# Seven depthwise jobs as seven block products each, and the block sums of h made in the value stage

## The chip, the cores and the metric

The kernel runs on one core of a Trainium2 chip. Time is the device's, in microseconds (us), from the first to the last instruction of one execution; several executions give a median. PE is TensorE, DVE is VectorE, ACT is ScalarE, POOL is GpSimd, and SP is the queue of SyncE, which here only issues transfers.

## The reference

Two transformer blocks on one sequence of 512 rows of width 1024. What the change touches is in the first block, here cut to it:

```
h = rmsnorm(x, pre_g) * (1 + sc) + sh                  # 512 x 1024
parts = split(h @ w_in)                                # b_gate, c_gate, x_in, z_a, q, k, v, z_b, g_a, g_b
q, k = rope(q), rope(k)
attn = neighbourhood_attention(q, k, v, k_ctx, v_ctx, rpb)
y_a = (silu(z_a) * b_gate * dwconv3(c_gate * x_in, conv_w, conv_b)) @ w_out_conv
y_b = (silu(z_b) * attn) @ w_out_attn
y = (sigmoid(g_a) * y_a + sigmoid(g_b) * y_b) @ w_o
x = x + gt * rmsnorm(y, post_g)
```

`dwconv3` is a depthwise convolution over three neighbouring rows. The second block (differential and forget-gate attention, memory attention, an MLP) follows and is not changed.

## The kernel before

All weights come as jobs of 1 MB: 1024 rows by 256 columns, as a tile `raw` of 128 partitions x 8 x 256. Each matmul operand is held as a high part (rounded to fp32r) and a low part (the rest), and a product is three matmuls: high by high, high by low, low by high (`mm3`). So a job is split before use: ACT makes the high part `wh` (`split_hi`, L314) and DVE or POOL the low part `wl` (`split_job`, L320). `raw`, `wh` and `wl` have two buffers each, so the split of a job runs while PE works on the job before it. SP loads `raw` in the order of the jobs, each load behind the split of the job two before (L418, L419).

An ordinary job (`tiles_job`) makes two output tiles of 128 x 512, each from 8 x 3 matmuls of 512 columns, into the two PSUM banks `acc`. A job as seven block products (`seven`) cuts weights and data into 2 x 2 blocks and makes seven products of 4 x 3 matmuls of 256 columns where eight would be needed. For that DVE makes four sums of weight blocks (`weight_sums`), ACT their high parts (`sums_hi`) and DVE their low parts (`sums_lo`), POOL makes the low parts of three plain weight blocks (`quads_lo`), and DVE puts the products together (L2053 to L2080). It also needs four sums of blocks of the data, split once for all its jobs.

The stages of the first block run in this order. **Value stage**: four jobs of six groups each (`token_group`, 24 matmuls of 256 columns into one bank); ACT evacuates each group (L1173), and stands between group 1 and group 2 to make the high part of the next job. **QK and attention**, with POOL making the rope sums and biases. **Depthwise stage**: sixteen jobs in turns of four (c_gate, x_in, b_gate, z_a), all ordinary, in loops of the hardware; job 0 is spread over the last attention steps. POOL meanwhile scales four gate weight tiles and sums them (L2542, L2549); nothing needs these sums before the next stage. **z_b stage**, four ordinary jobs. **Gate stage**: eight ordinary output jobs and then eight jobs g_a and g_b as seven products; POOL makes the sums of h (`gate_combos`, L2569 to L2578) while the output jobs run, from the high and the low part of h added again.

In SP's queue stand, after the first loads: a wait for h (`h_ready`) and for a small memset by POOL (`relb_ready`), seven small loads of tables, and then the loop of weight loads from value job 2 on. The tables go to `farena`, where x0 (from which h is made) lay; the tables are used after the value stage.

Of the kernel before, what the change touches and what calls it, by code (L numbers as in the profile page):

```python
# [8 lines left out]
SEQ = 512  # L9
KT = D // 128  # L10
GW, GR = 64, 8
CTX = 256
# [58 lines left out]
def build(nc, A, out):  # L71
# [3 lines left out]
    with ctx:  # L75
# [13 lines left out]
        small = sb("small", [128, 176])  # L89
# [14 lines left out]
        rarena = sb("rarena", [128, R_KB * 256], f32r)  # L104

# [26 lines left out]
        kx = [R(104, SEQ + 128 + CTX), R(111, SEQ + 128 + CTX)]  # L132
        cin = R(32, KT, SEQ)
        og = R(64, KT, SEQ)
        merged = R(96, KT, SEQ)
        wmod_a = view(early, 0, (8, KT, 256))
# [25 lines left out]
        hquads, hcombos = view(early, 32, (2, 2, 4, 256)), view(early, 48, (4, 4, 256))  # L162
        ht = view(rarena, 32, (4, 4, 256)), view(rarena, 48, (4, 4, 256))
# [33 lines left out]
        p1_t, u_q, w_q, v_q = F(16, 256), F(17, 256), F(18, 256), F(19, 256)  # L197
# [85 lines left out]

        def gate_home(c):
            kb = 112 if c == 0 else (76, 64)[c % 2]
            return tuple(view(rarena, kb + 6 * x, (3, 4, 128)) for x in range(2))
# [4 lines left out]

        def s_job(it, q0, c):
            return it * 4 + (14 + 4 * q0 + c)

        def acts(sj):
            return sj * 2 - 20
# [89 lines left out]
        def _(sp):  # L386
# [18 lines left out]
            sp.wait_ge(s_("h_ready"), KT)  # L405
            sp.wait_ge(s_("relb_ready"), 1)
# [26 lines left out]
        def _(pe):  # L433
# [420 lines left out]
            hold(pe, "xc_lo", 4)  # L854
            for c in range(8):
                seven(0, base + 8 + c, g + 16 + 2 * c, c, gate_home(c), gate_x)
# [6 lines left out]
            late_rows(0, JB["WO"], GB["WO"], merged, "merged_ready", 0)  # L863
            for c in range(1, 4):
                tiles_job(0, 2, JB["WO"] + c, 2, GB["WO"] + 2 * c, merged, between=memory_sum if c == 2 else None)
# [129 lines left out]
            for i in range(6):  # L995
                seven(0, JB["GO2"] + 6 + i, GB["GO2"] + 20 + 2 * i, 8 + i, gate2_home(i), gate2_x)
# [93 lines left out]
        def _(act):  # L1090
# [176 lines left out]
            def conv_turn(it, turn):  # L1267
                jb, gb, m0 = JB["CONV"] + 4 * turn, GB["CONV"] + 8 * turn, 2 * turn
                for c in range(4):
                    if c == turn == 0:  # L1270
                        split_hi(act, it, 4, jb + 2)
                        continue
                    if c == 1 - turn:
                        act.wait_ge(s_("gate_free"), it + turn + 1)
                        act.dma_start(gate_w, A["gate"][bass.ds(it + turn, 1)].rearrange("a p k n -> (a p) k n")
                                      if turn else A["gate"][0]).then_inc(s_("gate_in"), 16)
                    for t in range(2):
                        g = gb + 2 * c + t
                        if c == 0:
                            conv_first(it, turn, t)  # L1280
                        if c == 1:
                            wait_evacuated(act, it, 8, g)
                            f(y_t[:, t], u_t[:, t], ACT.Identity, bias=par[:, bass.ds(it * 2 + (P_CB + m0 + t), 1)],
                              scale=par[:, bass.ds(it * 2 + (P_CW + 8 + m0 + t), 1)]).then_inc(s_("tap_ready"), 1)
                        if c == 3:
                            acc_wait_ready(act, it, 8, g)
                            f(sg_t[:, t], acc[g % 2][:], ACT.Sigmoid).then_inc(s_("zsig_ready"), 1)
                    if c == 2:
                        acc_wait_ready(act, it, 8, gb + 5)
                    if c < 3:  # L1290
                        split_hi(act, it, 4, jb + c + 2)
                for t in range(2):
                    act.wait_ge(s_("cinf_ready"), it * 2 + (m0 + t + 1))
                    f(cin[0][:, bass.ds(it * 2 + (m0 + t), 1)].rearrange("p a n -> p (a n)"), y_t[:, t], ACT.Copy)\
                        .then_inc(s_("cin_hi"), 1)
                split_hi(act, it, 4, jb + 5)

            conv_turn(0, 0)
            with act.Fori(0, 3) as it:
                conv_turn(it, 1)  # L1300
# [25 lines left out]
            def prepare_first(it, base):  # L1326
                s = base % 2
                act.wait_ge(s_(f"raw_loaded{s}"), loads(it, base))
                f(wh[:, s, :, 0:128], raw[:, s, :, 0:128], ACT.Copy)
                f(quadrant(wh[:, s], 1, 1), quadrant(raw[:, s], 1, 1), ACT.Copy).then_inc(s_("hi_done"), 1)  # L1330

            def sums_hi(base, sj, home):
                for n in range(4):
                    hold(act, "sums_ready", sj * 4 + (2, 3, 3, 4)[n])
                    f(sum_home(0, base, n, home), bank(SUMS[n]), ACT.Copy).then_inc(c_("wsum_hi"), 1)

            def copy_p1(g, sj):
                hold(act, "prod_done", sj * 5 + 1)
                f(p1_t, acc[g % 2][:, 0:256], ACT.Copy).then_inc(c_("p1_copied"), 1)

# [14 lines left out]
            def merged_hi(c):  # L1355
                for t in (1, 0):
                    act.wait_ge(s_("mf_ready"), 2 * c + 2 - t)
                    f(merged[0][:, 2 * c + t], ya[:, 2 * c + t], ACT.Copy).then_inc(s_("merged_hi"), 1)
# [3 lines left out]
            for c in range(8):  # L1362
                if c < 7:
                    split_hi(act, 0, 2, jb + c + 1)
                else:
                    prepare_first(0, jb + 8)
                    sums_hi(jb + 8, 0, gate_home(0))
# [4 lines left out]
                if c == 5:  # L1372
                    hold(act, "combo_ready", 8)
                    for n in (0, 2, 1, 3):
                        f(ht[0][:, n], hcombos[:, n], ACT.Copy).then_inc(c_("xc_hi"), 1)
            for c in range(8):
# [3 lines left out]
                copy_p1(g, c)  # L1380
                if c < 7:
                    sums_hi(base, c + 1, gate_home(c + 1))
                else:
                    split_hi(act, 0, 2, base)
                quads_through(0, g, c, ACT.Sigmoid, lambda t: None)
# [211 lines left out]
            for n in range(4):  # L1597
# [5 lines left out]
                else:  # L1603
                    prepare_first(0, base + 1)
                    sums_hi(base + 1, 8, gate2_home(0))
# [4 lines left out]
                for u in range(4):  # L1610
# [5 lines left out]
                    for x in {(1, 3): (0, 2), (2, 0): (1,), (2, 1): (3,)}.get((n, u), ()):  # L1616
                        hold(act, "combo_ready", 16)
                        f(ht2[0][:, x], hcombos2[:, x], ACT.Copy).then_inc(c_("xc_hi"), 1)
            for i in range(6):
                base, g, sj = JB["GO2"] + 7 + i, GB["GO2"] + 20 + 2 * i, 8 + i  # L1620
                if i < 5:
                    prepare_first(0, base)
                copy_p1(g, sj)
# [100 lines left out]
            def finish(t, c, it, q0, sj):  # L1724
                hold(act, "relu_done", sj * 2 + 2 - t)
# [4 lines left out]
            def seven(it, c, q0, jb, gb):  # L1730
# [3 lines left out]
                copy_p1(g, sj)  # L1734
# [13 lines left out]
            def combos_hi(*which):  # L1748
                for x, made in which:
                    if made:  # L1750
                        hold(act, "combo_ready", 16 + made)
# [33 lines left out]
        def _(v):  # L1785
# [182 lines left out]

            v.wait_ge(s_("lo_done"), JB["CONV"] + 2)
            with v.Fori(0, 4) as it:  # L1970
                own.loop(it, 4)
                for c in range(4):
                    g = GB["CONV"] + 2 * c
                    if c == 0:
                        acc_wait_ready(v, it, 8, g + 1)
                    for t in range(2):
                        if c == 1:
                            wait_evacuated(v, it, 8, g - 2 + t)
                            acc_wait_ready(v, it, 8, g + t)
                            free_acc(tt(u_t[:, t], acc[(g + t) % 2][:], c_t[:, t], MUL), g + t)  # L1980
                        if c == 2:
                            v.wait_ge(s_("tap_ready"), it * 2 + (t + 1))
                            u, yy = u_t[:, t], y_t[:, t]
                            w0 = par[:, bass.ds(it * 2 + (P_CW + t), 1)]
                            w2 = par[:, bass.ds(it * 2 + (P_CW + 16 + t), 1)]
                            stt(yy[:, GR:], u[:, 0:SEQ - GR], w0, yy[:, GR:], MUL, ADD)
                            link(stt(yy[:, 1:GR], u[:, SEQ - GR:SEQ - 1], w0, yy[:, 1:GR], MUL, ADD))
                            stt(yy[:, 0:SEQ - GR], u[:, GR:], w2, yy[:, 0:SEQ - GR], MUL, ADD)
                            link(stt(yy[:, SEQ - GR:SEQ - 1], u[:, 1:GR], w2, yy[:, SEQ - GR:SEQ - 1], MUL, ADD))
# [828 lines left out]
```

## Time and profile before

| what | value |
|---|---|
| median of 3 runs | 1704.83 us (1703.72 to 1706.7) |
| span of the profiled execution | 1703.5 us |
| PE busy | 1661.9 us, 98% |
| DVE, ACT, POOL busy | 55%, 45%, 37% |
| instructions | 26528 |

The profiled execution is one of its own; its span is 1.3 us under the median of the runs. A line of the program such as L314 is named as in the profile. Busy time of PE is modelled at the ends of its matmuls, so it says where PE stood, not how well it was used.

### The profile page before, as it was taken

To read this page: it belongs to the slowest core of one execution; us is meant where nothing else is said; L and a number is where in the kernel's file an instruction comes from. 1 tells how busy PE (TensorE), PEld (TensorE's weight loads), DVE (VectorE), ACT (ScalarE), POOL (GpSimd) and SP (SyncE) were. 2 spreads that over 40 slices of the span, in tenths; PEclk is the share of its full clock that TensorE was granted. 3 is DMA by queue.
4 is the path that set the end of the run, shared out by engine and by line. 5 is a ranking of instruction groups with operands and counts; after the bars stand their busy time and mean duration, and the time that the engine had idled before them with its cause. 6 is when DMAs were issued, how large, how long until landed. Compare 5 with 4: busy or idle time off the path is not lost. (4 is left out here: it accounts for less than half of the span.)

```text
span 1703.5 us, 26528 instructions
## 1 busy us (share of the span) xinstructions
PE 1661.9 (98%) x10010; PEld 1408.0 (83%) x10010; DVE 940.9 (55%) x1657; ACT 764.6 (45%) x1326; POOL 631.7 (37%) x439
## 2 busy tenths in 40 slices
PE   6999999999999999999999999999999999999998
PEld 4987777778888889978987788798787788989896
DVE  5326566544445258847546664777545565555552
ACT  5324554532223234566545655444445324535351
POOL 1027767342220086643113332965100227323242
PEclk9999999999999999999999999999999999999998
DMA  7322122133333223345632110224411222222221
GB/s 323 112 88 68 55 74 80 63 129 123 106 116 123 99 83 102 105 179 189 233 119 80 50 50 30 96 100 177 169 50 52 98 99 99 100 99 98 99 100 50
DMA packets 29802, 181.68 MB, mean 107 GB/s; under 512 B 3352, under 2 KB 5784, under 8 KB 10112
## 3 DMA queue, kind: packets, MB, share of 16 engines
q1 hardware_dynamic: 22136, 150.12, 24.5%
q10 hardware_dynamic: 7560, 30.09, 5.1%
q8 instruction: 73, 1.20, 0.3%
q14 instruction: 33, 0.27, 0.1%
HBM read 169.57 MB, written 10.50 MB: 106 GB/s over the span
## 5 line engine op out<-in xcount | busy, mean ns | idle before, releaser
L438 PE MATMUL acc<-rarena,wh 128*128 128x512 f32 (+1 forms) x1720 | 657.7, 382 | 6.9 <-DVE rarena L1792 1.3
L440 PE MATMUL acc<-rarena,wl 128*128 128x512 f32 (+1 forms) x1720 | 642.3, 373 | 0.0
L439 PE MATMUL acc<-rarena,wh 128*128 128x512 f32 (+1 forms) x1720 | 641.9, 373 | 0.0
L438 PEld LDWEIGHTS acc<-rarena,wh 128*128 128x128 f32 x1720 | 323.9, 188 | 87.7 <-issue 23.5
L440 PEld LDWEIGHTS acc<-rarena,wl 128*128 128x128 f32 x1720 | 323.8, 188 | 62.1
L439 PEld LDWEIGHTS acc<-rarena,wh 128*128 128x128 f32 x1720 | 324.2, 188 | 56.4 <-issue 0.5
L320 DVE TENSOR_TENSOR wl<-raw,wh 128x2048 fp32r<-128x2048 f32 x81 | 197.2, 2434 | 239.7 <-ACT wh L314 239.6
L314 ACT ACTIVATE wh<-raw 128x2048 fp32r<-128x2048 f32 x99 | 188.9, 1908 | 76.0 <-PE acc L440 69.4
L2555 POOL TENSOR_TENSOR wl<-raw,wh 128x512 fp32r<-128x512 f32 x78 | 105.0, 1375 | 91.2 <-ACT wh L1330 91.2
L320 POOL TENSOR_TENSOR wl<-raw,wh 128x2048 fp32r<-128x2048 f32 x18 | 82.6, 4591 | 149.4 <-ACT wh L314 149.4
L516 PE MATMUL acc<-wh,rarena 128*128 128x256 f32 x336 | 94.2, 280 | 2.7 <-DVE rarena L1792 2.5
L517 PE MATMUL acc<-wl,rarena 128*128 128x256 f32 x336 | 94.1, 280 | 0.0
L518 PE MATMUL acc<-wh,rarena 128*128 128x256 f32 x336 | 94.0, 280 | 0.0
L2610 POOL TENSOR_TENSOR farena<-farena 128x512 f32<-128x512 f32 x34 | 52.4, 1541 | 110.5 <-ACT farena L1646 51.0
L2318 DVE TENSOR_TENSOR farena<-acc,farena 128x512 f32<-128x512 f32 x48 | 33.1, 689 | 89.9 <-PE acc L440 89.7
L1792 DVE TENSOR_TENSOR rarena<-T,rarena 128x512 fp32r<-128x512 f32 (+3 forms) x116 | 64.6, 563 | 23.6 <-ACT rarena L1532 11.1
L1939 DVE CUSTOM_DVE_ANT_1 S<-S,farena 128x512 f32<-128x512 f32 x64 | 43.2, 715 | 59.1 <-PE S L657 59.1
L2542 POOL TENSOR_SCALAR farena<-farena,small 128x256 f32<-128x256 f32 x32 | 32.5, 1036 | 99.9 <-DMA farena<-in_gate 99.9
L2569 POOL TENSOR_TENSOR early<-rarena 128x1024 f32<-128x1024 f32 x8 | 23.0, 2909 | 117.2 <-PE acc L440 117.2
L516 PEld LDWEIGHTS acc<-wh,rarena 128*128 128x128 f32 x336 | 63.3, 188 | 3.5 <-issue 3.2
L2555 POOL TENSOR_TENSOR rarena<-farena,rarena 128x512 fp32r<-128x512 f32 x31 | 41.7, 1345 | 65.0 <-ACT rarena L1728 62.4
L1346 ACT ACTIVATE farena<-farena 128x512 f32<-128x512 f32 x26 | 16.4, 633 | 108.7 <-DVE farena L2075 81.7
(346 smaller groups left out, 3083.2 us busy)
## 6 DMA issues: line engine op xcount, KB each, us to landing
raw<-in_w SPq DMA_DIRECT2D x129, 1024.0 KB, 4.8
early<-in_wmod SPq DMA_DIRECT2D x8, 1024.0 KB, 19.8
farena<-in_gate ACTq DMA_DIRECT2D x4, 1024.0 KB, 4.8
mkv_scratch<-rarena ACTq DMA_DIRECT2D x2, 2048.0 KB, 12.0
rarena<-mkv_scratch ACTq DMA_DIRECT2D x1, 4096.0 KB, 15.0
farena<-in_rpb ACTq DMA_DIRECT2D x16, 240.0 KB, 3.8
farena<-in_x_grid SPq DMA_DIRECT2D x2, 1024.0 KB, 6.9
o_scratch<-early ACTq DMA_DIRECT2D x8, 256.0 KB, 2.0
```

The source lines that it names most:

```text
L314: nc.scalar.activation(wh[:, s], raw[:, s], ACT.Copy).then_inc(s_("hi_done"), 1)
L320: eng.tensor_tensor(wl[:, s], raw[:, s], wh[:, s].bitcast(f32), ALU.subtract)\
L438: mm(o, w[0], m[0], start=start, stop=False)
L439: mm(o, w[0], m[1], start=False, stop=False)
L440: return mm(o, w[1], m[0], start=False, stop=stop)
L516: mm(o, st[0], wh[:, s, k], start=k == 0, stop=False)
L517: mm(o, st[0], wl[:, s, k], start=False, stop=False)
L518: last = mm(o, st[1], wh[:, s, k], start=False, stop=k == KT - 1)
L1792: return tt(dst, src, hi.bitcast(f32), SUB)
L1939: nc.vector.tensor_tensor_reduce(S[a][:], S[a][:], bias, -1.0, 3.0e38, ADD, MIN, negmax[:, cc:cc + 1])\
L2555: return gt(dst, a, b.bitcast(f32), SUB)
L2610: gt(dst, dst, src, ADD).then_inc(s_(name), 1)
```

## The change

- Of the depthwise jobs, numbers 3, 4, 7, 8, 11, 12 and 15 (`CONV_FAST`: all four z_a jobs and three of the four c_gate jobs) become seven products. Their weight sums, low parts and put-together work are added to ACT, DVE and POOL in this stage, and the loops are written out.
- The four sums of h for block products are made once, by POOL in the value stage, right behind the four seam copies, from x0 itself. ACT makes their high parts between the evacuations of value job 1, and POOL their low parts. They serve the depthwise and the gate stage; the gate stage's own sums (twelve POOL operations and four ACT copies) go.
- SP waits for these sums (`combo_ready`, 4) before the table loads, since they read x0.
- POOL's rows of gate weights (`gate_rows`) follow the low parts of jobs 4, 8, 12 and 15 in place of running on their own.
- A tile `extra` of 16 KB in each partition holds high parts; for it the space for software DMA descriptors is cut to 64 bytes. Some other tiles move.

```diff
+        hsums = [view(crown, 4 * n, (4, 256)) for n in range(2)] + [view(early, 56 + 4 * n, (4, 256)) for n in range(2)]
+        ht = view(extra, 0, (4, 4, 256)), view(rarena, 112, (4, 4, 256))
...
+        CONV_FAST = (3, 4, 7, 8, 11, 12, 15)
...
 # SP
             sp.wait_ge(s_("h_ready"), KT)
+            hold(sp, "combo_ready", 4)
             sp.wait_ge(s_("relb_ready"), 1)
             sp.dma_start(relb[0:32, 0:4], A["rel_bias"]).then_inc(s_("relb_in"), 16)
...
 # PE
-            with pe.Fori(0, 3) as it:
-                for c in range(1, 5):
-                    tiles_job(it, 4, JB["CONV"] + c, 8, GB["CONV"] + 2 * c, h)
-            for c in range(13, 16):
-                tiles_job(0, 4, JB["CONV"] + c, 8, GB["CONV"] + 2 * c, h)
+            hold(pe, "xc_lo", 4)
+            for c in range(1, 16):
+                base, g = JB["CONV"] + c, GB["CONV"] + 2 * c
+                if c in CONV_FAST:
+                    seven(0, base, g, CONV_FAST.index(c), conv_home(c), gate_x)
+                else:
+                    tiles_job(0, 4, base, 8, g, h)
...
 # ACT, value stage
                     free_acc(f(dst[:, JW * c:JW * c + JW], acc[g % 2][:, 0:JW], ACT.Copy), g)
+                    if c == 1 and gi > 1:
+                        n = gi - 2
+                        hold(act, "combo_ready", n + 1)
+                        f(ht[0][:, n], hsums[n], ACT.Copy).then_inc(s_("h_hi"), 1)
...
 # ACT, depthwise stage
+            for c in range(2, 17):
+                m, kind = divmod(c, 4)
+                acc_wait_ready(act, 0, 8, gb + 2 * c - 1)
+                if kind == 2:
+                    taps(m)
+                if kind == 0:
+                    z_sigmoid(m - 1)
+                if c + 1 in CONV_FAST:
+                    prepare_first(0, jb + c + 1)
+                if c in CONV_FAST:
+                    copy_p1(gb + 2 * c, CONV_FAST.index(c), conv_sums[0])
+                if c + 1 in CONV_FAST:
+                    sums_hi(jb + c + 1, CONV_FAST.index(c + 1), conv_home(c + 1))
+                else:
+                    split_hi(act, 0, 4, jb + c + 1)
+                if kind == 0:
+                    cin_hi(m - 1)
+                if kind == 2:
+                    load_gate(m)
...
 # DVE, depthwise stage
+            def fast_conv(c, dst, first, pending):
+                sj = CONV_FAST.index(c)
+                seven(0, jb + c + 1, gb + 2 * c, sj, conv_home(c + 1) if c + 1 in CONV_FAST else None,
+                      lambda: None, first, pending, dst=(dst[:, 0], dst[:, 1]), sums=conv_sums)
...
+            for m in range(4):
+                if m > 0:
+                    fast_conv(4 * m, c_t, lambda: gated_conv(m - 1), lambda: cin_lo(m - 1))
+                acc_wait_ready(v, 0, 8, gb + 8 * m + 1)
+                split_job(v, 0, 4, jb + 4 * m + 2)
+                for t in range(2):
+                    g = gb + 8 * m + 2 + t
+                    wait_evacuated(v, 0, 8, g - 2)
+                    acc_wait_ready(v, 0, 8, g)
+                    free_acc(tt(u_t[:, t], acc[g % 2][:], c_t[:, t], MUL), g)
+                weight_sums(0, jb + 4 * m + 3, CONV_FAST.index(4 * m + 3))
+                sums_lo(jb + 4 * m + 3, CONV_FAST.index(4 * m + 3), conv_home(4 * m + 3), 0, 1, 2, 3)
+                taps(m)
+                fast_conv(4 * m + 3, z_t, lambda: None, lambda: None)
+            gated_conv(3)
+            split_job(v, 0, 4, jb + 17)
+            cin_lo(3)
...
 # POOL, value stage
             gp.wait_ge(s_("h_ready"), KT)
-            nc.gpsimd.memset(relb[0:32], 0.0).then_inc(s_("relb_ready"), 1)
             for n in range(2):
                 for dst, src in ((slice(0, 64), slice(SEQ - 64, SEQ)), (slice(64, 128), slice(0, 64))):
                     nc.gpsimd.tensor_copy(hseam[n][:, :, dst], h[n][:, :, src]).then_inc(s_("seam_ready"), 1)
...
+            hb = [x0[:, 4 * j:4 * j + 4, 256 * l:256 * l + 256] for j in range(2) for l in range(2)]
+            gt(hsums[0], hb[B11], hb[B12], SUB).then_inc(c_("combo_ready"), 1)
+            hold(gp, "combo_ready", 1)
+            gt(hsums[1], hsums[0], hb[B22], ADD).then_inc(c_("combo_ready"), 1)
+            gt(hsums[2], hb[B12], hb[B22], SUB).then_inc(c_("combo_ready"), 1)
+            hold(gp, "combo_ready", 2)
+            gt(hsums[3], hb[B21], hsums[1], SUB).then_inc(c_("combo_ready"), 1)
+            hold(gp, "combo_ready", 4)
+            nc.gpsimd.memset(relb[0:32], 0.0).then_inc(s_("relb_ready"), 1)
+            for n in range(4):
+                gp.wait_ge(s_("h_hi"), KT + n + 1)
+                minus(ht[1][:, n], hsums[n], ht[0][:, n]).then_inc(c_("xc_lo"), 1)
...
 # POOL, depthwise stage
+            for sj, c in enumerate(CONV_FAST):
+                quads_lo(0, JB["CONV"] + c, sj)
+                if c % 4 == 0:
+                    gate_rows(c // 4 - 1)
+            gate_rows(3)
...
-            gp.wait_ge(s_("acc_ready"), GB["GO"] + 8)
-            gate_combos(0, hquads, hcombos, gate_x, ht)
-            quads_lo(0, JB["GO"] + 8, 0)
+            quads_lo(0, JB["GO"] + 8, NCF)
```

## Rows read from the trace of the kernel before

**Rows 1.** The page: span, and busy time by engine.
```profile
span 1703.5 us, 26528 instructions
...
PE 1661.9 (98%) x10010; PEld 1408.0 (83%) x10010; DVE 940.9 (55%) x1657; ACT 764.6 (45%) x1326; POOL 631.7 (37%) x439
```
**Rows 2.** PE's waits, whole span and depthwise stage: total us, times, longest.
```profile
PE O L547 <- DMA early<-in_wmod: 12.2, 1, 12.2
...
PE acc L438 <- DVE farena L1991: 0.9, 1, 0.9
```
**Rows 3.** PE by stretches: us, busy (matmuls), granted clock, DMA share, GB/s.
```profile
374.80:419.60 44.80, 44.80 (x194) 1.00 0.33 113
639.70:720.50 80.80, 80.24 (x673) 1.00 0.28 96
1110.60:1174.50 63.90, 61.36 (x505) 1.00 0.29 103
1435.40:1475.50 40.10, 40.10 (x337) 1.00 0.30 106
```
**Rows 4.** DVE in time, depthwise stage, first and second turn: start, us.
```profile
351.37 2.87 DVE L1986 SCALAR_TENSOR_TENSOR farena<-farena,par 128x504 f32<-128x504 f32 x1
...
397.46 0.74 DVE L1986 SCALAR_TENSOR_TENSOR farena<-farena,par 128x504 f32<-128x504 f32 x1
```
**Rows 5.** DVE in time, a gate job's sums and the last gate job.
```profile
650.37 1.13 DVE L2033 TENSOR_TENSOR T<-raw 128x512 f32<-128x512 f32 x1
...
658.02 0.68 DVE L1792 TENSOR_TENSOR wl<-O,wh 128x512 fp32r<-128x512 f32 x1
...
718.19 2.28 DVE L320 TENSOR_TENSOR wl<-raw,wh 128x2048 fp32r<-128x2048 f32 x1
```
**Rows 6.** POOL in time, depthwise stage: the three sums of a gate tile.
```profile
430.93 4.72 POOL L2549 TENSOR_TENSOR farena<-farena 128x1024 f32<-128x1024 f32 x3
```
**Rows 7.** POOL in time: seam copies; first and last of four sums of h.
```profile
48.07 2.28 POOL L2466 CAST rarena<-rarena 128x512 fp32r<-128x512 f32 x4
...
606.73 2.42 POOL L2573 TENSOR_TENSOR early<-early 128x1024 f32<-128x1024 f32 x1
...
615.99 2.39 POOL L2578 TENSOR_TENSOR early<-early 128x1024 f32<-128x1024 f32 x1
```
**Rows 8.** DVE in time: the splits beside these POOL operations.
```profile
48.96 3.53 DVE L320 TENSOR_TENSOR wl<-raw,wh 128x2048 fp32r<-128x2048 f32 x1 [1.10 <-ACT wh L314]
...
608.74 2.56 DVE L320 TENSOR_TENSOR wl<-raw,wh 128x2048 fp32r<-128x2048 f32 x1 [6.68 <-ACT wh L314]
```
**Rows 9.** SP in time: first table load; first of three weight loads.
```profile
48.20 0.34 SPq L407 DMA_DIRECT2D farena<-in_rel_bias  x1
...
51.65 14.23 SPq L419 DMA_DIRECT2D raw<-in_w  x3
```
**Rows 10.** DMA issues, us to landing: whole run; value jobs 2 and 3.
```profile
raw<-in_w SPq DMA_DIRECT2D x129, 1024.0 KB, 4.8
...
raw<-in_w SPq DMA_DIRECT2D x1, 1024.0 KB, 6.9
...
raw<-in_w SPq DMA_DIRECT2D x1, 1024.0 KB, 8.5
```
**Rows 11.** ACT in time, value job 1: split, groups 2 and 3.
```profile
61.02 1.91 ACT L314 ACTIVATE wh<-raw 128x2048 fp32r<-128x2048 f32 x1
63.57 0.39 ACT L1173 ACTIVATE early<-acc 128x256 f32<-128x256 f32 x1 [0.64 <-PE acc L518]
66.39 0.38 ACT L1173 ACTIVATE early<-acc 128x256 f32<-128x256 f32 x1 [2.44 <-PE acc L518]
```
**Rows 12.** PE by stretches at the end, columns as in rows 3.
```profile
1690.00:1692.00 2.00, 1.34 (x12) 1.00 0.00 0
...
1694.00:1696.00 2.00, 2.00 (x15) 0.69 0.00 0
1696.00:1700.00 4.00, 0.40 (x2) 0.50 0.71 268
```

More of the change, by code:

```diff
@@ L196, in build @@
         mt = [F(20, SEQ), F(22, SEQ)]
-        p1_t, u_q, w_q, v_q = F(16, 256), F(17, 256), F(18, 256), F(19, 256)
+        p1_t, u_q, w_q, v_q = late_sums = F(16, 256), F(17, 256), F(18, 256), F(19, 256)
+        conv_sums = tuple(view(upper, n, (256,)) for n in range(4))
+        z_t = view(upper, 4, (2, SEQ))
         eps = small[:, 0:1]
@@ L1264, in _ @@
             spill_o(0, 7, 7, 0)
[L1267 to L1291, printed above, removed]
-                for t in range(2):
[L1293 to L1296, printed above, removed]
@@ L1323, in _ @@
                     load_o(c + 2)
[L1326 to L1339, printed above, removed]
             def quads_through(it, g, sj, func, then, scaled=None):
@@ L2005, in _, with weight_sums @@
-            own.done(4)
+            def weight_sums(it, base, sj):
+                r = raw[:, base % 2]
+                v.wait_ge(s_(f"raw_loaded{base % 2}"), loads(it, base))
+                hold(v, "wsum_lo", sj * 4)
+                tt(bank(SUMS[0]), quadrant(r, 1, 0), quadrant(r, 1, 1), ADD).then_inc(c_("sums_ready"), 1)
+                hold(v, "sums_ready", sj * 4 + 1)
+                tt(bank(SUMS[1]), bank(SUMS[0]), quadrant(r, 0, 0), ADD).then_inc(c_("sums_ready"), 1)
+                hold(v, "sums_ready", sj * 4 + 2)
+                tt(bank(SUMS[2]), bank(SUMS[1]), quadrant(r, 0, 1), ADD).then_inc(c_("sums_ready"), 1)
+                tt(bank(SUMS[3]), quadrant(r, 0, 0), quadrant(r, 1, 0), ADD).then_inc(c_("sums_ready"), 1)
@@ new lines, in sums_lo, with seven @@
+            def sums_lo(base, sj, home, *which):
+                for n in which:
+                    hold(v, "wsum_hi", sj * 4 + n + 1)
+                    lo(sum_home(1, base, n, home), bank(SUMS[n]), sum_home(0, base, n, home)).then_inc(c_("wsum_lo"), 1)
+            def seven(it, base, g, sj, home, quads_free, first, pending, scale=None, dst=mt, sums=late_sums):
+                p1_t, u_q, w_q, v_q = sums
+                if home:
+                    weight_sums(it, base, sj + 1)
+                first()
+                hold(v, "prod_done", sj * 5 + 2)
+                hold(v, "p1_copied", sj + 1)
+                hold(v, "combined", sj * 5)
+                tt(u_q, S[0][:, 0:256], p1_t, SUB).then_inc(c_("combined"), 1)
+                hold(v, "prod_done", sj * 5 + 3)
+                hold(v, "combined", sj * 5 + 1)
+                tt(w_q, u_q, acc[1 - g % 2][:, 0:256], SUB).then_inc(c_("combined"), 1)
+                if home:
+                    sums_lo(base, sj + 1, home, 0)
+                hold(v, "prod_done", sj * 5 + 4)
+                tt(v_q, S[1][:, 0:256], u_q, ADD).then_inc(c_("combined"), 1)
+                hold(v, "combined", sj * 5 + 2)
+                quads_free()
+                tt(dst[1][:, 256:512], S[1][:, 0:256], w_q, ADD).then_inc(c_("combined"), 1)
+                if home:
+                    sums_lo(base, sj + 1, home, 1, 2)
+                acc_wait_ready(v, it, 16, g)
+                free_acc(tt(dst[0][:, 0:256], acc[g % 2][:, 0:256], p1_t, ADD), g)
+                if home:
+                    sums_lo(base, sj + 1, home, 3)
+                else:
+                    split_job(v, it, 8, base)
+                pending()
+                hold(v, "prod_done", sj * 5 + 5)
+                hold(v, "combined", sj * 5 + 3)
+                tt(dst[1][:, 0:256], S[0][:, 0:256], v_q, ADD).then_inc(c_("combined"), 1)
+                if scale:
+                    hold(v, "combined", sj * 5 + 5)
+                    tt(mt[1], mt[1], rstd, MUL).then_inc(c_("scaled"), 1)
+                acc_wait_ready(v, it, 16, g + 1)
+                free_acc(tt(dst[0][:, 256:512], acc[1 - g % 2][:, 0:256], w_q, SUB), g + 1)
+                wait_evacuated(v, it, 16, g + 1)
```

258 lines of the change are left out of this document (113 added, 145 removed).

## The prediction

> **What bounds the kernel now.** I read the page's engine line first: TensorE (PE) is busy in 98% of the span of 1703.5 us [rows 1]. I then read its waits: outside the first 12.2 us, when it waits for the first modulation weights, each named cause is a few microseconds at most, and in the depthwise stage there is one wait in all, 0.9 us [rows 2]. So every matmul that goes is time won, and every wait put in front of PE is time lost. The windows by stage give the price of a job. Four ordinary depthwise jobs take 44.8 us, 11.20 each, with PE busy throughout. A job as seven block products takes 80.8 / 8 = 10.10 in the first block's gate stage, 40.1 / 4 = 10.03 in an MLP quarter, and 63.9 / 6 = 10.65 in the second block's gate stage, where VectorE (DVE) and POOL carry more work around it and PE loses 2.5 us to waits [rows 3]. This agrees with the count: 84 matmuls of 256 columns do the work of 42 of 512 instead of 48.
>
> **What the depthwise stage gains.** Seven jobs at 11.20 - 10.05 = 1.15 us give 8.0 us. The bounds come from the same rows: 8.2 (at 10.03) and 3.9 (at 10.65). The one wait there is PE held by L1991, the product of convolution and gate. It was late because the tap before it took 2.87 us where the same line takes 0.74 later [rows 4]; POOL's gate sums ran beside it. In the new order the first gate rows come behind the first two fast jobs' low parts, so this wait goes: another 0.9 us, in the sums 1.0.
>
> **What it adds there.** A fast job's weight sums and low parts take DVE 8.3 us from the first sum at 650.37 to the end of the last low part at 658.70 [rows 5]. Before a job 4m+3 they start 0.7 us into the job before (behind the last x product) and are done by about 7 us of its 11.2, so they are covered. The taps after them reach some 1.7 us into job 4m+3, whose second bank is first needed by its third product, at 2 x 1.43 = 2.9 us: covered. Job 4m+3 must make the sums for job 4m+4, starting 1.7 us late: 1.7 + 8.3 = 10.0, against a job of 10.05. This has no cover left; I take 0 to 0.6 us three times, 0.5 in all.
>
> Tighter is the end of each job 4m+4, and of job 15. Its successor is an ordinary job, and the DVE split of that job's weights stands inside the seven-product routine behind the fifth product. That is the order in the last gate job of before: the split takes 2.28 us, from 718.19 to 720.47 [rows 5], and PE goes on right then. It just fits with POOL quiet. Here POOL is not quiet: gate rows now follow the low parts of jobs 4, 8, 12 and 15, and their three sums take 4.72 us [rows 6], some 2.4 of it in the first, falling about where this split stands. A DVE operation with two SBUF operands beside such a sum waited 2.87 - 0.74 = 2.1 us [rows 4]. I take 0.7 us for jobs 4, 8 and 12 each and 1.4 for job 15, whose gate rows start latest: 3.5 in all, bounds 0 (POOL between two sums) and 4 x 2.1 = 8.4. With the 0.5 that is 4.0. The stage's net is -8.0 - 1.0 + 4.0 = -5.0 us; bounds -9.2 and +4.
>
> ScalarE's added copies there stand where its timeline is idle, and no more operations pass per job than in the gate stage, which runs at 10.10. Taking the four sums out of the gate stage wins nothing: PE has no wait at its first block product there. The unrolled loops I price at 0: the loops' boundaries show no PE wait, and neither do the straight-line stages. The smaller DMA scratch I also price at 0: all data queues on the page are hardware queues before, and the transfers keep their issuing engines.
>
> **What moving the sums costs.** This decides. POOL makes the four sums of h behind h_ready, and SyncE (SP) must wait for all four before it issues seven table loads, since one of them lands on x0. Behind these, in the same queue, stands the weight load of value job 2. Step by step:
> - POOL's four seam copies start when h is ready and end at about 50.2 [rows 7]. It then makes four dependent 128x1024 sums. The same four in the gate stage ran from 606.73 to 618.38: 11.65 us, with one DVE weight split of 2.56 in between. A split stands here too, at 48.96 [rows 7, 8]. Without the collision they would be 4 x 2.4 = 9.6. So the sums end at 61.9 (60.0 at the least).
> - SP's first table load now goes out at 48.20, 0.3 us behind the release; then 62.2. Job 2's load is issued 3.45 us after the first (51.65 - 48.20): 65.65 [rows 9].
> - It landed in 6.9 us behind these same tables; 4.8 is the run's median and 8.5 the next load's [rows 10]. Landing: 72.55. Before it was 58.55, 2.5 us ahead of its use.
> - ScalarE takes it at 61.02, between the evacuations of groups 1 and 2 of value job 1, and its order is fixed: 1.91 us of split and then the evacuation at 63.57 [rows 11]. Now it stands at that split until 72.55, and the evacuation of group 2 ends at 74.9. PE has two banks; group 3 fills the second by 66.4, and group 4 needs the first. So PE stands from 66.4 to 74.9: 8.5 us. Bounds: with 9.6 and 4.8 in place of 11.65 and 6.9 it is 4.4; with 8.5 it is 10.1.
>
> Behind it nothing more is late: job 3's load follows at once and is used a pass later; the added high copies (about 1 us each) stand between evacuations that have 2.4 us to spare; POOL's low parts end some 25 us before its first rope work; the tables are used after 105 us.
>
> A pause of this length also touches the granted clock. At the end of the run it is 1.00 (2.4 GHz) while matmuls are dense, 0.69 on average in 1694 to 1696, a few microseconds after the last dense ones, and 0.50 (1.2 GHz) after that [rows 12]. A pause in mid-kernel stands in no row. One group of 24 matmuls takes 2.83 us (66.39 - 63.57 [rows 11]) and would take about twice that at half the level; I take somewhat less than one group, 2.0 us more, with bounds 0 (no fall) and 5.7 (two groups).
> The Trainium skill ("TensorE: Matmul & The Clock Gate", Part 1: The HAM clock gate) says that an idle PE drops to half rate and must be kept busy again to come back. By that the term is above 0, as I take it; if the row's fall belongs to the end of the program only, the sum is 2.0 lower. No run here shows it yet.
>
> **The sum.** +8.5 + 2.0 - 5.0 = +5.5 us on the profiled 1703.5: 1709.0. The median of the runs, 1704.83, is 1.3 above that execution; I forecast 1710.0 for the median.
>
> **The rivals.**
> 1. *The two sides cancel.* The pause is as I price it, but the clock stays up and the depthwise stage takes no new waits: 8.5 - 9.0 = -0.5, some 1704. For it: the gate stage runs seven-product jobs nearly without waits. Against: its POOL has no gate rows, and the fall of the clock in the one pause that rows show.
> 2. *Faster: the late load is mostly covered.* The sums meet no DVE split and the load lands in 4.8 us; the pause is 4.4, with the clock up: 4.4 - 9.0 = -4.6, some 1700. Below about 5.6 us of pause, with no new waits, it ends faster beyond what a measurement can tell, 0.2% or 3.4 us. Against: the split does stand there, and the tables do go ahead in the queue.
> 3. *DVE becomes the depthwise stage's bound.* Jobs run at 10.65, as in the second gate stage, and the collisions come on top: -3.9 - 1.0 + 4.0 = -0.9; with +10.5 in the value stage that is +9.6, some 1714. For it: DVE has no slack in jobs 4m+3 and 4m+4. Against: two ordinary jobs in each four let it catch up.
>
> **How the numbers follow.** Forecast 0.50, rival 1 0.22, rival 2 0.13, rival 3 0.15. The range leaves out the outer halves of rivals 2 and 3 and the tails: 1700.5 to 1716. The likeliest case's own is 1706 to 1714. Slower by over 0.2% is rival 3 and all but 0.07 of the forecast: 0.58; same is rival 1 with that 0.07, less 0.02 of rival 1 on the fast side: 0.27; faster is rival 2 and that 0.02: 0.15.
>
> **What would show it.** In the profile after: SP's first table load at about 62 instead of 48; ScalarE's split of value job 2 released by the load at 71 to 74; one PE wait of 5 to 10 us near 70, with a granted clock below 1.00 behind it; two fast depthwise jobs in each four at 10 to 10.7 us. The forecast is wrong if value job 2's load lands before 64, or if PE waits in the depthwise stage come to more than 8 us.

## The result, and the profile after

The changed kernel takes 1693.08 us (median of 5 runs, 1689.21 to 1694.6), against 1704.83 us (1703.72 to 1706.7, also 5 runs and not 3): ratio 0.9927, 95% interval 0.9914 to 0.9939. It is 0.7% faster. The forecast was 1710.0, slower, with a range of 1700.5 to 1716; the time lies below the range and on the side that had a chance of 0.15.

What had been forecast for the value stage did happen. On POOL the seam copies and the first and last of the four sums, and on SP the first table load and the late weight loads (start in us, duration; the answers to [rows 7, 9]):

```profile
49.37 4.36 POOL L2505 CAST rarena<-rarena 128x512 fp32r<-128x512 f32 x4 [23.97 <-DVE rarena L1816]
53.70 2.41 POOL L2511 TENSOR_TENSOR crown<-farena 128x1024 f32<-128x1024 f32 x1
...
60.90 2.40 POOL L2516 TENSOR_TENSOR early<-farena,crown 128x1024 f32<-128x1024 f32 x1
```
```profile
63.65 0.34 SPq L419 DMA_DIRECT2D farena<-in_rel_bias  x1
...
67.09 0.93 SPq L431 DMA_DIRECT2D raw<-in_w  x2
```

ScalarE (ACT) in time behind it, the answer to [rows 11], and PE's longest waits, which answer to [rows 2] (us in total, times, longest):

```profile
62.73 0.38 ACT L1186 ACTIVATE early<-acc 128x256 f32<-128x256 f32 x1 [2.50 <-PE acc L530]
73.26 1.91 ACT L325 ACTIVATE wh<-raw 128x2048 fp32r<-128x2048 f32 x1 [10.15 <-DMA raw<-in_w]
75.08 0.37 ACT L1186 ACTIVATE early<-acc 128x256 f32<-128x256 f32 x1
```
```profile
PE O L559 <- DMA early<-in_wmod: 11.5, 1, 11.5
PE acc L528 <- ACT early L1186: 7.1, 1, 7.1
```

The load of value job 2 goes out at 67.09 and frees ScalarE's split at 73.26. ScalarE stands 10.15 us at it, the evacuation behind it is late, and PE stands 7.1 us, the longest wait after the start. PE by stretches (us, busy and matmuls, granted clock, DMA share, GB/s), first around this pause, then the first four jobs that the depthwise stage runs in its new order (two ordinary ones, two of seven products, and the gap behind them):

```profile
57.00:66.00 9.00, 9.00 (x77) 1.00 0.05 13
66.00:73.00 7.00, 2.45 (x21) 1.00 0.97 350
73.00:80.00 7.00, 4.50 (x21) 0.53 0.37 136
80.00:87.00 7.00, 7.00 (x60) 0.99 0.27 112
```
```profile
345.53:367.47 21.94, 21.94 (x99) 1.00 0.40 142
367.47:387.62 20.15, 20.15 (x169) 1.00 0.19 70
387.62:388.18 0.56, 0.16 (x3) 1.00 0.00 0
```

The clock is at 0.53 on average behind the pause, so it does fall to its lower level, 1.2 GHz, in mid-kernel. The seven-product jobs take 10.08 us, as forecast. But the two ordinary jobs, whose code is unchanged, take 10.97 each, where four of them took 11.20 each in [rows 3]. That is the surprise, and it is not confined to this stage. Six matmuls of an ordinary job, as PE starts them:

```profile
351.83 0.39 PE L450 MATMUL acc<-rarena,wh 128*128 128x512 f32 x1
352.05 0.39 PE L451 MATMUL acc<-rarena,wh 128*128 128x512 f32 x1
352.28 0.39 PE L452 MATMUL acc<-rarena,wl 128*128 128x512 f32 x1
352.51 0.39 PE L450 MATMUL acc<-rarena,wh 128*128 128x512 f32 x1
352.73 0.39 PE L451 MATMUL acc<-rarena,wh 128*128 128x512 f32 x1
352.96 0.39 PE L452 MATMUL acc<-rarena,wl 128*128 128x512 f32 x1
```

Five steps take 1.13 us, 0.226 each; before, a step takes 11.20 / 48 = 0.233. Such a step, from one matmul's start to the next one's, is called the pace below. Over the whole run, from the starts in the trace (steps over 0.3 us, where PE waits or changes its work, left out), 512-column matmuls stand 0.2279 us apart, before 0.2333; 256-column ones 0.1202, before 0.1187 (steps under 0.18). There are some 3,650 of the former and 4,450 of the latter, so at equal numbers this is 3650 x 0.0054 = 19.7 us less and 4450 x 0.0015 = 6.7 more: 13 us, in a change that touches few of them.

### The profile page after: what moved, and what is told of

Same layout as the page of the kernel before. It is cut to its first block and busy times, and to the rows that moved or that the text cites. A ratio compares the mean times of both kernels' runs of the same rounds, so it can differ in the third digit from the quotient of the medians.

```text
span 1692.8 us, 27072 instructions
## 1 busy us (share of the span) xinstructions
PE 1646.1 (97%) x10262; PEld 1423.6 (84%) x10262; DVE 978.4 (58%) x1755; ACT 775.3 (46%) x1362; POOL 648.4 (38%) x456
## 5 line engine op out<-in xcount | busy, mean ns | idle before, releaser
L450 PE MATMUL acc<-rarena,wh 128*128 128x512 f32 (+1 forms) x1664 | 623.7, 375 | 6.9 <-ACT farena L1637 1.3
L451 PE MATMUL acc<-rarena,wh 128*128 128x512 f32 (+1 forms) x1664 | 607.0, 365 | 0.0
L452 PE MATMUL acc<-rarena,wl 128*128 128x512 f32 (+1 forms) x1664 | 606.9, 365 | 0.0
L450 PEld LDWEIGHTS acc<-rarena,wh 128*128 128x128 f32 x1664 | 313.9, 189 | 77.7 <-issue 23.8
L452 PEld LDWEIGHTS acc<-rarena,wl 128*128 128x128 f32 x1664 | 313.9, 189 | 51.5
L451 PEld LDWEIGHTS acc<-rarena,wh 128*128 128x128 f32 x1664 | 314.3, 189 | 45.0 <-issue 0.5
L331 DVE TENSOR_TENSOR wl<-raw,wh 128x2048 fp32r<-128x2048 f32 x74 | 179.0, 2418 | 207.7 <-ACT wh L325 207.5
L2508 POOL TENSOR_TENSOR wl<-raw,wh 128x512 fp32r<-128x512 f32 x99 | 131.8, 1358 | 293.7 <-ACT wh L1288 291.6
L325 ACT ACTIVATE wh<-raw 128x2048 fp32r<-128x2048 f32 x92 | 175.6, 1908 | 68.8 <-PE acc L452 52.3
L1816 DVE TENSOR_TENSOR rarena<-T,rarena 128x512 fp32r<-128x512 f32 (+3 forms) x130 | 73.9, 576 | 30.3 <-ACT rarena L1556 11.2
L1963 DVE CUSTOM_DVE_ANT_1 S<-S,farena 128x512 f32<-128x512 f32 x64 | 43.2, 715 | 58.6 <-PE S L669 58.6
L451 PE MATMUL acc<-rarena 128*128 128x256 f32 x264 | 74.7, 283 | 0.0
L451 PE MATMUL S<-rarena,wh 128*128 128x256 f32 x264 | 74.7, 283 | 0.0
```

The costliest lines, as they stand in the source:

```text
L325: nc.scalar.activation(wh[:, s], raw[:, s], ACT.Copy).then_inc(s_("hi_done"), 1)
L331: eng.tensor_tensor(wl[:, s], raw[:, s], wh[:, s].bitcast(f32), ALU.subtract)\
L450: mm(o, w[0], m[0], start=start, stop=False)
L451: mm(o, w[0], m[1], start=False, stop=False)
L452: return mm(o, w[1], m[0], start=False, stop=stop)
L1816: return tt(dst, src, hi.bitcast(f32), SUB)
```

## The experiments

**Which part of the diff changes the pace.** The diff moves tiles. One line of it was too small to be quoted ahead: the tile `small` grows from 176 to 184 columns, of which no new one is used. Tiles lie one behind the other in each partition, so `farena` and `rarena`, which come after it, move by 32 bytes against the tiles before it. By the layout of the built programs `rarena` starts at byte 98144 before, 32 past a multiple of 64, and at 81856 after, a multiple; `wh` and `wl` start at a multiple in both. The other candidate was the smaller space for software DMA descriptors. Each was tried alone in the kernel before, and the first was undone in the changed one.

`b_small184`:
```diff
-        small = sb("small", [128, 176])
+        small = sb("small", [128, 184])
```


> The kernel before with one edit: the tile small gets 8 more unused columns, 32 bytes in each partition, so that farena and rarena, which lie behind it, start at a multiple of 64 bytes as they do after the change (before: 32 past one). Theory A (the place of rarena sets the pace of matmuls that stream 512 columns from it): the start-to-start time of such matmuls falls from 0.233 to 0.227 us, and with some 4,150 of them the time falls by 20 to 27 us, to 1678 to 1685. Theory B (the faster pace comes from the smaller DMA scratch, from the code that is written out, or from another chip or day): pace 0.233 and 1704 to 1706.

Measured: 1687.72 us, ratio to before 0.9897 (0.9878 to 0.9917), 512-column steps of 0.2277 us. The pace is that of theory A, the time is not: 16 us less instead of 20 to 27. Theory A's sum left out the 256-column matmuls. With them, 3,990 x 0.0056 = 22 us less and 3,880 x 0.0015 = 6 more come to 16.

`b_scratch64`, the kernel before with the descriptor space alone cut to 64 bytes:

> The kernel before with one edit: the space for software DMA descriptors is 64 bytes. All tiles move down by 16,320 bytes, a multiple of 64. Theory A: pace of the 512-column matmuls 0.233 us, time within 4 us of 1704.8. Theory B, if the scratch is the cause: pace 0.227 us, 1678 to 1685. If it is this that made the matmuls of 256 columns slower (0.118 or 0.119 to 0.120 us), they show 0.120 here and the time rises by 2 to 5 us.

Measured: 1703.15 us, ratio 0.9999 (0.9987 to 1.0011), steps of 0.2333. It does nothing.

`a_small176`, the changed kernel with the old size:
```diff
-        small = sb("small", [128, 184])
+        small = sb("small", [128, 176])
```


> The changed kernel with small at its old width, so that farena and rarena lie 32 bytes past a multiple of 64; everything else of the change stays. Theory A: the pace goes back to 0.233 us for about 3,820 matmuls, +20 to +24 us on the changed kernel: 1712 to 1718, which is slower than before by what the pause in the value stage costs less what the seven jobs give. Theory B: 1691 to 1695, as the changed kernel.

Measured: 1705.15 us, ratio to before 1.0006 (0.9995 to 1.0017), steps of 0.2333; below the 1712 to 1718 of theory A, for the same reason as above. Eight unused columns are worth 1% to the kernel before, and the rest of the change, taken together, is worth nothing that the run times can tell. This kernel is also where the prediction's terms can be read at the old pace:

```profile
PE acc L528 <- ACT early L1186: 8.2, 1, 8.2
```
```profile
65.56 0.28 PE L530 MATMUL acc<-wh,rarena 128*128 128x256 f32 x1
74.07 0.58 PE L528 MATMUL acc<-wh,rarena 128*128 128x256 f32 x1 [8.23 <-ACT early L1186]
...
79.28 0.28 PE L528 MATMUL acc<-wh,rarena 128*128 128x256 f32 x1
...
351.64 0.40 PE L450 MATMUL acc<-rarena,wh 128*128 128x512 f32 x1
...
352.34 0.40 PE L450 MATMUL acc<-rarena,wh 128*128 128x512 f32 x1
```
```profile
344.53:367.04 22.51, 22.51 (x98) 1.00 0.40 146
367.04:387.05 20.01, 20.01 (x169) 1.00 0.16 61
387.05:387.75 0.70, 0.15 (x3) 1.00 0.00 0
```

The first rows are PE's wait in the value stage. Then come, in order of time, the matmuls before and behind it, the one 24 matmuls later, and two that lie three passes apart in an ordinary job, 0.70 us or 0.233 a step. The last rows are the same four jobs as above: 11.26 for an ordinary one, 10.00 for one of seven products, and a stretch of 0.70 in which PE stands 0.55 for DVE's split.

**Which tile it is.** Four more layouts of the kernel before.

`b_small192`, with `small` at 192 columns (64 bytes more than before):

> The kernel before with the tile small at 192 columns: every later tile moves by 64 bytes, so the large tile that the matmuls stream from starts again 32 bytes past a multiple of 64. Theory A (the start of that tile modulo 64 bytes sets the pace): 512-column matmuls stay at 0.233 us start to start, and the time is that of before, 1702 to 1706 us. Rival B (any move of the tiles, or a wider small, is enough): 0.227 us and about 1688 us, as with 184 columns.

Measured: 1704.1 us, ratio 1.0001 (0.9992 to 1.0011). It is not any move that helps.

`b_pad_rarena`:
```diff
         farena = sb("farena", [128, int(F_KB * 256)])
+        pad = sb("pad", [128, 8])
```


> The kernel before with small at 176 columns, and 32 empty bytes between the two large tiles: farena stays 32 bytes past a multiple of 64, rarena starts at a multiple. Theory A1 (it is rarena alone, from which the three-pass matmuls stream): 0.227 us, 1685 to 1690 us. Theory A2 (it is farena, which DVE, ACT, POOL and the DMA queues work on): 0.233 us, 1702 to 1706 us. Both have a part in it: between, about 1695 us.

Measured: 1688.56 us, ratio 0.9912 (0.9896 to 0.9929).

`b_farena_only`, with the same line and `small` at 184:

> The mirror of the last one: small at 184 columns and 32 empty bytes between the two large tiles, so farena starts at a multiple of 64 and rarena 32 bytes past one. Theory A1 (rarena alone): 0.233 us, 1702 to 1706 us. Theory A2 (farena): 0.227 us, 1685 to 1690 us.

Measured: 1704.47 us, ratio 1.0005 (0.9996 to 1.0015), steps of 0.2333, against 0.2276 in `b_pad_rarena`. So `rarena` is the tile and `farena` has no part in it. From `rarena` the matmuls stream; the weights come from `wh` and `wl`.

`b_pad_wh`:
```diff
         raw = sb("raw", [128, 2, KT, JW])
+        pad = sb("pad", [128, 8])
         wh = sb("wh", [128, 2, KT, JW], f32r)
```


> The kernel before with 32 empty bytes ahead of the weights' tile wh: wh, wl, the parameters, identity and ones start 32 bytes past a multiple of 64, small, farena and rarena at a multiple. If only the tile that the 512-column matmuls stream counts: they stand at 0.227 us, as with small at 184. If the weights' place counts as well: 512-column matmuls (weights stationary) differ from 0.227 us. The 256-column matmuls that stream wh were at 0.118 us with rarena 32 bytes off and at 0.120 us with it at a multiple; if it is the distance between the two operands that counts there, they go to 0.118 us here again. Time 1680 to 1692 us by the first, above 1700 us by the second.

Measured: 1703.9 us, ratio 1.0002 (0.9992 to 1.0011), steps of 0.2333. My theory up to here, that the start of the streamed tile alone sets the pace, is wrong: `rarena` starts at a multiple of 64 in this kernel and the pace is the old one. The weights' place counts too.

**Distance or start.** Two layouts to tell whether it is the distance of the two operands or the start of each.

`b_both32`, with the line of `b_pad_wh` and `small` at 184:

> The kernel before with 32 empty bytes ahead of wh and small at 184 columns: the weights' tiles wh and wl and the two large tiles all start 32 bytes past a multiple of 64. Theory D (what counts is the distance of the weights' tiles from rarena modulo 64 bytes: 32 in the kernel before, 0 in the fast ones, 32 again with the weights alone moved): 512-column matmuls at 0.227 us, 1685 to 1690 us. Theory E (each of the two tiles has to start at a multiple of 64): 0.233 us, 1702 to 1706 us.

Measured: 1688.64 us, ratio 0.9907 (0.9888 to 0.9926), steps of 0.2278. With weights and `rarena` both 32 bytes off, the pace is the better one. So theory E, a multiple of 64 for each tile, is out, and it is the distance that counts (theory D), though not in the simple way that the next run asks about.

`b_pad_wl`:
```diff
         wh = sb("wh", [128, 2, KT, JW], f32r)
+        pad = sb("pad", [128, 8])
         wl = sb("wl", [128, 2, KT, JW], f32r)
```


> The kernel before with 32 empty bytes between wh and wl: wh starts at a multiple of 64, wl, farena's neighbours and farena itself as they come (wl 32 past, farena and rarena at a multiple). Of the three passes of a product two take their weights from wh and one from wl. If the collision is one of a single matmul's two operands (theories D and E), one pass in three is slow: 0.227, 0.227 and 0.233 us, about 1692 us. If one pass is slowed by the weights that are loaded meanwhile for the next, it is another of the three, with the same sum. If the tiles' places act on all matmuls together, all three are at 0.233 us (1702 to 1706 us) or all at 0.227 us (1685 to 1690 us).

Measured: 1704.21 us, ratio 1.0001 (0.9991 to 1.001). The sum of one slow pass in three, 0.687 us, is not what came; three passes take 0.700, as with all three slow. Yet the passes differ. The second and third pass of the 512-column products, in `b_pad_wl`, in `b_pad_wh` and in `b_both32` (L440 takes its weights from `wh`, L441 from `wl`; matmuls, busy us, mean ns of one):

```profile
L440 PE MATMUL acc<-rarena,wh 128*128 128x512 f32 x1384 | 552.0, 399 | 0.0
L441 PE MATMUL acc<-rarena,wl 128*128 128x512 f32 x1384 | 539.7, 390 | 0.0
```
```profile
L441 PE MATMUL acc<-rarena,wl 128*128 128x512 f32 x1384 | 547.3, 395 | 0.0
L440 PE MATMUL acc<-rarena,wh 128*128 128x512 f32 x1384 | 547.1, 395 | 0.0
```
```profile
L441 PE MATMUL acc<-rarena,wl 128*128 128x512 f32 x1384 | 539.8, 390 | 0.0
L440 PE MATMUL acc<-rarena,wh 128*128 128x512 f32 x1384 | 539.6, 390 | 0.0
```

395 is the mark of the old pace and 390 that of the better one. In `b_pad_wl` the pass at 390 is the one whose own weights are off, and the one before it, during which those weights are loaded, is the longest, at 399. That load and that pass, from the rows of PE's weight loads (PEld) and of PE:

```profile
351.82 0.40 PE L440 MATMUL acc<-rarena,wh 128*128 128x512 f32 x1
...
351.83 0.19 PEld L441 LDWEIGHTS acc<-rarena,wl 128*128 128x128 f32 x1
```

By the starts in the trace (medians) the passes step by 0.233, 0.239 and 0.228. So a matmul isn't slowed just by the distance of its own two operands. Nor is it slowed just by that of the weights loaded meanwhile: the first pass is slow too, although its own weights and those loaded during it both come from `wh`, which lies to `rarena` as in the better layouts. What holds over all kernels of this study is a rule for the three tiles together:

| kernel | start of wh, wl / farena / rarena, modulo 64 | 512-column step, us | ratio to before |
|---|---|---|---|
| before | 0, 0 / 32 / 32 | 0.2333 | 1 |
| b_scratch64 | 0, 0 / 32 / 32 | 0.2333 | 0.9999 |
| a_small176 | 0, 0 / 32 / 32 | 0.2333 | 1.0006 |
| a_lf_small176 | 0, 0 / 32 / 32 | 0.2333 | 0.9958 |
| b_small192 | 0, 0 / 32 / 32 | 0.2333 | 1.0001 |
| b_farena_only | 0, 0 / 0 / 32 | 0.2333 | 1.0005 |
| b_pad_wh | 32, 32 / 0 / 0 | 0.2333 | 1.0002 |
| b_pad_wl | 0, 32 / 0 / 0 | 0.2332 | 1.0001 |
| this change | 0, 0 / 0 / 0 | 0.2279 | 0.9927 |
| b_small184 | 0, 0 / 0 / 0 | 0.2277 | 0.9897 |
| b_pad_rarena | 0, 0 / 32 / 0 | 0.2276 | 0.9912 |
| b_both32 | 32, 32 / 32 / 32 | 0.2278 | 0.9907 |
| a_loads_first | 0, 0 / 0 / 0 | 0.2279 | 0.9861 |
| a_lf_gate_wait | 0, 0 / 0 / 0 | 0.2279 | 0.9867 |

All tiles that PE reads in these products at one offset modulo 64: the better pace, six times of six. One of them 32 bytes against the others: the old pace, eight times of eight. The 256-column steps part the same way, 0.1202 in the six and 0.1185 to 0.1189 in the eight. But these are fewer cases than fourteen. By the same layouts `rarena` starts 65,280 bytes behind `wh` in all six; in the others it starts 65,248 or 65,312 bytes behind it, or, in `b_pad_wl`, 65,280 with `wl` 32 bytes off. 65,280 is a multiple of 256 too, so "modulo 64" is a guess: no run has another multiple of 64 at the better pace. Why the chip does so stays open.

**The pause, and the depthwise stage by itself.** The load of value job 2 doesn't need the sums. `a_loads_first` is the changed kernel with this edit in SP's order:
```diff
-            load_job(1)
+            for j in range(1, 4):
+                load_job(j)
...
-            with sp.Fori(0, (NJ - 2) // 2) as it:
+            with sp.Fori(1, (NJ - 2) // 2) as it:
```


> The changed kernel with the weight loads of value jobs 2 and 3 issued by SP ahead of its wait for the sums, and the loop of loads from job 4 on. If the pause of 7.1 us near 70 is this load alone, it goes, the granted clock stays at 1.00 there, and the time falls by 8 to 10 us (7.1 of pause and some 2 of matmuls at half the clock): 1683 to 1686. If something else is late next (the sums for ScalarE's copies, the low part of the job), a wait of some us stays and the gain is under 5 us.

Measured: 1681.02 us, ratio to before 0.9861 (0.9842 to 0.988); 11 us less than the change by the two ratios, 12 by the medians, where 8 to 10 were expected. The pause and the fall of the clock are gone; the same stretches as above, in this kernel:

```profile
66.00:73.00 7.00, 7.00 (x60) 1.00 0.82 290
73.00:80.00 7.00, 7.00 (x61) 1.00 0.00 1
```

`a_lf_small176` is this kernel with `small` at 176 again:

> The changed kernel with the loads of value jobs 2 and 3 issued ahead of the wait for the sums, and small back at 176 columns, so at the old addresses. Theory A (three effects that add up: addresses, pause, depthwise stage): the pause and its fall of the clock are gone and the depthwise stage keeps its gain of about 8 us, with 512-column matmuls at 0.233 us: 1704 - 8 - about 2 = 1694 us (1692 to 1697). Rival (the earlier loads gave their gain only together with the new addresses): 1700 us or more.

Measured: 1696.57 us, ratio 0.9958 (0.9944 to 0.9972), 0.42% or 7 us below before. By the ratios the pause with its clock costs 8 us at the old pace (0.9958 to 1.0006) and 11 at the new one (0.9861 to 0.9927), and what the change was written for gives 7. The effects add up only to about 3 us, and part of that is the start of an execution. In the fourteen traces the first record of the granted clock, at 1.00, stands at 20.5 to 36.3 us, and PE's 257th matmul, early in the value stage, starts at 43.2 to 48.0, in groups that follow that rise (last section). POOL's seam copies, in `a_loads_first` and in `a_lf_gate_wait` below, which are alike up to there:

```profile
49.19 4.35 POOL L2506 CAST rarena<-rarena 128x512 fp32r<-128x512 f32 x4 [23.91 <-DVE rarena L1817]
...
44.75 4.36 POOL L2506 CAST rarena<-rarena 128x512 fp32r<-128x512 f32 x4 [19.30 <-DVE rarena L1817]
```

Counted in the traces from the last matmul before the pause to the point where the clock is up again, and against the same matmuls in the kernel without it, the pause with its clock costs 10.8 us at the old pace and 9.3 at the new one.

`a_lf_gate_wait` is `a_loads_first` with one wait more on POOL, ahead of the gate sums:
```diff
                 if c % 4 == 0:
+                    gp.wait_ge(s_("lo_done"), JB["CONV"] + c + 2)
                     gate_rows(c // 4 - 1)
```


> The changed kernel with the earlier loads, in which POOL holds the gate sums of a column group until DVE has split the weights of the next depthwise job. Theory of the prediction (DVE's weight splits and POOL's sums hold each other up at jobs 4, 8 and 12, 0.7 us each): the waits of PE for the split tiles in the depthwise stage fall by up to 1 us in all; the time falls by 0 to 2 us against the kernel with the earlier loads alone (1681 us), within its scatter. Rival (the waits left come from the change of kind of job, at 15 to the next stage): they stay at 2.0 us in all.

Measured: 1680.69 us, ratio 0.9867 (0.9851 to 0.9883): no difference to `a_loads_first` that can be told. PE's waits for the split in the depthwise stage (330 to 530 us), without the wait on POOL and with it:

```profile
PE acc L451 <- DVE wl L331: 1.5, 2, 1.1
```
```profile
PE acc L451 <- DVE wl L331: 0.4, 1, 0.4
```

The 0.4 at job 4 is gone, and of 1.1 at job 15 there is 0.4 left, though nothing was changed at job 15. So only the 0.4 can be put down to the edit. Collisions of that kind are there; in these traces they come to 1.5 us at most. These two are the best kernels of the study, 1.3 to 1.4% below before.

## Why the prediction was wrong

**The step that failed** is the sum: "+8.5 + 2.0 - 5.0 = +5.5 us on the profiled 1703.5". It takes the rest of the span as it was. The work outside the touched stages is the same, but its pace is not, because a tile's size moved `rarena` against the weights. I listed that some tiles move and gave it no term, not even a zero with a reason. At the old addresses (`a_small176`) the time is 1705.15; at the new ones 1693.08. That is 12 us by the medians, 13 by the two ratios, and 13 worked out from the steps. It is what made the kernel faster. A second term, the collisions in the depthwise stage, was too large by some 3 us; it is among the terms below. [Rows 3] held the old pace, 44.80 us for 192 matmuls, and I used it as a constant of the chip.

**The terms, at the old pace** (stages and waits from `a_small176`, single instructions of the value stage from the change's profile above):
- *Pause of PE:* +8.5 forecast. In `a_small176` PE's matmuls at 65.56 and 74.07 lie 8.5 us apart where a step is 0.12: 8.4 measured. (The profile counts 8.2 as idle, and 7.1 at the new pace; both are within the bounds of 4.4 to 10.1.) The size is right in part by luck, since two parts erred against each other. The sums met no DVE split and took 4 x 2.4 = 9.6 as in the lower bound. But the seam copies before them took 4.36 us in place of 2.28: the split stood beside them instead (in the change at 50.41, for 2.29 us), and this time it was POOL that was held and not the split, which before took 3.53 [rows 8]. From the start of the copies to the end of the sums it is 13.9 us, where the forecast has 48.07 to 61.9, or 13.8. The load then took 6.2 us from issue to ScalarE's start in the change and 7.1 in `a_small176`, where 6.9 was forecast.
- *Clock:* +2.0 forecast, 2.4 measured: the 24 matmuls behind the pause take from 74.07 to 79.28, 5.2 us, where such a group takes 2.83 [rows 11]. The Trainium skill ("TensorE: Matmul & The Clock Gate", Part 1: The HAM clock gate) says that an idle PE drops to half rate; the 0.53 behind the pause agrees. With the pause the clock's 2.4 make 10.8 us. The first job of the depthwise stage's new order begins 10.25 us later than before (344.53 against 334.28), because this execution was 0.5 us ahead when the pause came.
- *Depthwise stage:* -5.0 net forecast, -8.3 measured. By PE's starts in the two traces the fifteen jobs of the new order take from 344.53 to 505.49, 161.0 us, and before from 334.28 to 503.52, 169.2. Seven jobs at 11.20 - 10.00 are 8.4, where 8.0 was forecast; the wait at L1991 is gone; and the 4.0 in the sum for late sums and for collisions of DVE with POOL shows as one wait of 0.6 us, behind job 4. I had moved the 2.1 us of one slowed DVE operation [rows 4] to four places where the split and POOL's sums only might meet. In the three kernels looked at (`a_small176`, the change and `a_loads_first`) such waits come to 0.6 to 1.5 us, behind jobs 4 and 15 alone. This term was mis-sized.

With these sizes the sum would have been 8.4 + 2.4 - 8.3 = +2.5 us, between the forecast and the first rival ("the two sides cancel"), and it would still have missed the 0.7%. That rival's condition, a clock that stays up, was not met. Rival 2, a pause mostly covered, didn't happen: the load went out at 67.09. Rival 3, jobs of 10.65, didn't either: 10.00 and 10.08. And the two signs by which the forecast was to be known wrong, a load that lands before 64 and waits of over 8 us in the depthwise stage, both failed to appear in a forecast that was wrong: they tested the terms in the sum and none that was missing from it.

What stays open: by which mechanism the distance of the tiles acts, above all why the three passes of `b_pad_wl` differ as they do, and at which other distances the better pace is had; it was seen at one alone, and all moves of these tiles against each other were by 32 or 64 bytes.

## What to carry to other kernels

When a change alters a tile's size or adds a tile, work out where every tile behind it moves, and compare the step of the same matmuls in a stage that the change doesn't touch before any other stage is read; a version that has the layout alone gives the rest of the change its true price, here nothing instead of 0.7%. Where PE reads weights and streamed data from tiles of their own, try them at a distance that is a multiple of 256 bytes, as 65,280 is; here the way there cost 32 bytes and gave 1%. A wait put into a DMA queue delays every load behind it: loads that don't need what it waits for go ahead of it, which gave another 9 to 12 us. And where two single traces are compared, take the difference of their starts out first; here it was up to 4.8 us.

## What the runs showed of the hardware

- 512-column fp32r matmuls step by 0.2277 us with `rarena` 65,280 bytes behind `wh` and 48,896 behind `wl` (`b_small184`), and by 0.2333 with 32 bytes less (before), 2.4% more, with nothing else changed. 256-column ones go the other way, 0.1202 and 0.1187. The better layout is also the steadier one: 95% of its 256-column steps are 0.119 to 0.121, while those of the other scatter from 0.115 to 0.122. The Trainium skill ("TensorE: Matmul & The Clock Gate", Part 2, Back-to-back issue gap) gives N/2.4 + 2.5 ns for an isolated matmul, an estimate of 216 ns at 512 columns; no layout here came to that, and the measured steps decide.
- A pause of 7.1 us in mid-kernel put TensorE's clock to its lower level (0.53 on average from 73 to 80 us). In `a_small176` a pause of 8.4 us cost 10.8 with the 2.4 at the lower clock behind it.
- The first record of the granted clock at 1.00, taken here as its first rise, came at 20.5 to 36.3 us in the fourteen traces, with PE at work since 11.3 to 12.2, and with it the value stage began at other times: PE's 257th matmul at 43.2 to 43.3 us after a rise at 20.5 to 20.7, at 45.5 to 46.4 after one at 26.4 to 29.1, and at 47.8 to 48.0 after one at 35.6 to 36.3. Where the clock rose at 21.3 and fell again from 28.1 to 34.9 (`b_small184`) it was 45.8.
